# Hybrid decoder trunk on one core: first tile's gates on its own columns, query weights scaled a stage earlier, state's copy ahead of the exponential, last tile's norm by halves

## The reference

```python
# first layer, both groups from one projection of h
c_q, k_a, v_a, k_i, w_i, q_b, z_f, i_b, g_b = split(h @ w_in)
q_a = rms_norm(c_q) @ w_uq                       # queries of the attention heads
# attention: per query the 256 best keys of an index score, softmax with ALiBi
logits = (q_a . k_a) * 64 ** -0.5 - slope_h * distance
# gated recurrence (HGRN2): forget gate and key from z, per channel
logf = log(sigmoid(z_f)); k_b = sigmoid(-z_f)    # lb of the one even layer is 0
S_t = exp(logf_t) * S_(t-1) + k_t v_t ;  o_t = q_t . S_t    # S starts at 0
o = concat(o_attention, rms_norm(o_recurrent) * silu(g_b)) @ w_out
# every block
h = layer_norm(ALPHA * h + block(h)) * g + b
```

## Time and profile before

| | |
|---|---|
| Median of 3 runs | 2665.35 us (2661.79 to 2667.26) |
| Profiled execution, its own time | 2666.79 us |
| Span of its trace | 2665.0 us, mean granted clock 0.967 |
| PE busy | 2548.1 us (96%) |
| DVE busy | 1290.3 us (48%) |
| ACT busy | 844.5 us (32%) |
| POOL busy | 1063.0 us (40%) |
| HBM read, written | 215.81 MB, 12.71 MB |

### The profile page before, as it was taken

How to read it: one execution, slowest core, us unless ns; L and a number is a source line. 1 busy time by engine, 2 the same in 40 slices (tenths; PEclk the granted TensorE clock), 3 DMA queues, 4 the chain that set the end, 5 groups by cost and what they waited for, 6 DMA issues and landing times.

```text
span 2665.0 us, 36229 instructions
## 1 busy us (share of the span) xinstructions
PE 2548.1 (96%) x14090; PEld 2180.5 (82%) x14090; DVE 1290.3 (48%) x2460; ACT 844.5 (32%) x1387; POOL 1063.0 (40%) x624
## 2 busy tenths in 40 slices
PE   7899999789999989999999999999999999999996
PEld 6789999667788778899888777888787888888885
DVE  6789999588886423333333323332232332232224
ACT  3675221333333223222222322322332322332221
POOL 0432213364544414344434433444433444455442
PEclk9899999699999999999999989999998999999998
DMA  4101220333233234333323223233322233333331
GB/s 133 32 17 43 89 92 19 99 92 116 87 107 96 88 103 119 96 95 95 87 72 95 80 63 95 65 110 95 95 79 79 79 101 103 94 91 103 113 103 46
DMA packets 274613, 230.87 MB, mean 87 GB/s; under 512 B 10640, under 2 KB 255440, under 8 KB 274448
## 3 DMA queue, kind: packets, MB, share of 16 engines
q1 hardware_dynamic: 266256, 220.07, 27.7%
q10 hardware_dynamic: 8192, 8.52, 0.9%
HBM read 215.81 MB, written 12.71 MB: 86 GB/s over the span
## 4 chain that ended last, share of the span: by engine, by line
PE 59%; DMA 1%; POOL 1%; DVE 1%; ACT 1%; issue 0%; POOLq 0%; SPq 0%; ACTq 0%; DVEq 0%
PE banks L1959 36%; PE banks L1975 20%; PE banks L1992 1%; PE banks L1997 1%; PE banks L2009 1%; DMA cq_raw<-in_w_up 0%; PE banks L1668 0%; DMA last_draw<-in_w_down 0%; POOL dL L1877 0%; POOL wL L1866 0%; POOL wL L1870 0%; PE banks L1994 0%; DVE y L1641 0%; DVE y L2165 0%; ACT dH L2059 0%
## 5 line engine op out<-in xcount | busy, mean ns | idle before, releaser
L1870 POOL TENSOR_TENSOR wL<-cq_raw,wH 128x2048 fp32r<-128x2048 f32 x87 | 405.7, 4664 | 565.7 <-ACT wH L2053 565.7
L1959 PE MATMUL banks<-hL,wH 128*128 128x512 f32 (+1 forms) x1760 | 618.9, 352 | 5.6 <-ACT hid L2068 5.3
L1959 PE MATMUL banks<-hH,wL 128*128 128x512 f32 (+1 forms) x1760 | 618.0, 351 | 0.0
L1959 PE MATMUL banks<-hH,wH 128*128 128x512 f32 (+1 forms) x1760 | 616.1, 350 | 0.0
L2145 DVE TENSOR_TENSOR hid<-hid,banks 128x512 f32<-128x512 f32 (+1 forms) x110 | 64.3, 585 | 742.8 <-PE banks L1959 639.2
L1959 PEld LDWEIGHTS banks<-hL,wH 128*128 128x128 f32 x1760 | 331.3, 188 | 54.9 <-ACT hid L2068 6.5
L1959 PEld LDWEIGHTS banks<-hH,wL 128*128 128x128 f32 x1760 | 331.2, 188 | 46.4
L1959 PEld LDWEIGHTS banks<-hH,wH 128*128 128x128 f32 x1760 | 331.8, 189 | 44.9
L1877 POOL TENSOR_TENSOR dL<-last_draw,dH 128x1024 fp32r<-128x1024 f32 x88 | 220.8, 2509 | 350.6 <-ACT dH L2059 350.6
L2165 DVE TENSOR_TENSOR y<-y,banks 128x512 f32<-128x512 f32 (+1 forms) x340 | 233.1, 686 | 219.9 <-PE banks L1975 218.8
L1975 PE MATMUL banks<-dH,hidL 128*128 128x512 f32 (+1 forms) x748 | 303.9, 406 | 2.3 <-issue 2.3
(11 more groups left out here) (249 smaller groups left out, 4248.0 us busy)
## 6 DMA issues: line engine op xcount, KB each, us to landing
cq_raw<-in_w_gate SPq DMA_DIRECT2D x88, 512.0 KB, 4.6
cq_raw<-in_w_up SPq DMA_DIRECT2D x88, 512.0 KB, 6.0
last_draw<-in_w_down SPq DMA_DIRECT2D x88, 512.0 KB, 3.4
w_out_part<-in_w_out SPq DMA_DIRECT2D x60, 512.0 KB, 4.0
va<-in_w_in SPq DMA_DIRECT2D x10, 1024.0 KB, 5.5
va<-in_x SPq DMA_DIRECT2D x8, 512.0 KB, 4.4
vg_scratch<-y ACTq DMA_DIRECT2D x32, 128.0 KB, 1.7
y<-in_x SPq DMA_DIRECT2D x8, 512.0 KB, 7.5
```

Of the source, the lines that this page charges most:

```text
L1870: nc.gpsimd.tensor_tensor(wL[:, ff % 2, :, :, :].rearrange("p g k f -> p (g k f)"), raw[:, :, :, :].rearrange("p g k f -> p (g k f)"), wH[ ...
L1959: last = nc.tensor.matmul(banks[:, GU + (2 * q + g) % 3, 0:n], wt[:, ff % 2, g, k, :], h[:, k, a:a + n], start=(k == 0 and part == 0), sto ...
```

## The change

Four edits.

1. **First tile's gates.** For tile 0 the gate sub-steps work on that tile's own 16 columns per 128 (64 of 512). The padding memsets of z and q on GpSimd and SP's waits for them go; VectorE sets one key buffer to zero instead, and `S` is set to zero behind the first gate step. For tile 0 `out` leaves out the products with the state, which is zero.
2. **Query weights.** They are loaded in the projection stage into a free row of y and scaled there by ScalarE, in front of its last eight evacuations. `qa` of tile 0 reads them there and is done first in the mixers' stage; a copy by DMA from SBUF to SBUF serves the other tiles. SP waits for the copy and for `qa` of tile 0 before it loads y.
3. **State's copy.** In step h = 3 ScalarE copies the state before the exponential, as it already did with the job of step 5.
4. **The end.** ScalarE copies the last gain row into two PSUM banks during phase 3; VectorE reads it from there. The last tile's gain and bias are both done by VectorE, by halves of 512 columns, and each half is stored by itself.

```diff
+w_qa0 = y[:, 2, :].rearrange("p (k f) -> p k f", k=QC)
 # projection, SP
             sp.dma_start(slab_raw(j), ...)
+            if j == len(SLABS) - 2:
+                sp.dma_start(w_qa0, ins["w_uq"][0]...).then_inc(w_qa_loaded, 16)
 # projection, ScalarE
                 out_of_bank(m)
+                if m == len(slab_units) - 8:
+                    act.wait_ge(w_qa_loaded, 16)
+                    for h in range(A_HEADS):
+                        at = w_qa0[:, :, h * HD:(h + 1) * HD]
+                        nc.scalar.activation(at, at, ACT.Copy, scale=HD ** -0.5 / SLOPES[h]).then_inc(w_qa_scaled, 1)
 # mixers, SP
-        sp.dma_start(w_qa[:, :, :], ins["w_uq"][0]...).then_inc(w_loaded, 16)
-        sp.wait_ge(pads, 1)
         load_z(0)
-        sp.wait_ge(pads, 2)
         load_q(0)
-        sp.wait_ge(pads, 5)
+        sp.dma_start(w_qa[:, :, :], w_qa0).then_inc(w_loaded, 16)
+        sp.wait_ge(pads, 3)
         load_v(0)
 ...
         n0.load(sp, ins["ln_mix_g"][0], ins["ln_mix_b"][0])
+        sp.wait_ge(w_loaded, 16)
+        sp.wait_ge(shared_psum, nth["qa", 0])
         for m in range(5):
             load_y(m)
 # mixers, GpSimd
-        nc.gpsimd.memset(zt[:, :], PAD_Z).then_inc(pads, 1)
-        nc.gpsimd.memset(qt[:, :], 0.0).then_inc(pads, 1)
-        nc.gpsimd.memset(qp[:], 0.0).then_inc(pads, 1)
         nc.gpsimd.memset(vt[:, 0, :], 0.0).then_inc(pads, 1)
         nc.gpsimd.memset(gt[:, :], 0.0).then_inc(pads, 1)
+        nc.gpsimd.memset(qp[:], 0.0).then_inc(pads, 1)
 # mixers, TensorE
-                        nc.tensor.matmul(..., qp[:, s, par, ...], state[...], start=True, stop=False)
+                        if m:
+                            nc.tensor.matmul(..., qp[:, s, par, ...], state[...], start=True, stop=False)
-                        last = nc.tensor.matmul(..., S[:, s, h, :], vt[...], start=False, stop=True)
+                        last = nc.tensor.matmul(..., S[:, s, h, :], vt[...], start=(m == 0), stop=True)
 ...
+        on_shared("qa", 0)
         gram(0, 0)
-        on_shared("qa", 0)
 # mixers, ScalarE
+            if m == 0:
+                z, ut, lt, kt, k_in, to = own(z), own(ut), own(lt), own(kt), own(k_in), own(to)
 ...
-        gates(0, 2)
-        gates(0, 3)
-        act.wait_ge(w_loaded, 16)
-        for h in range(4):
-            scaled(h)
-        gates(0, 4)
-        gates(0, 5)
-        for h in range(4, A_HEADS):
-            scaled(h)
+        for stage in (2, 3, 4, 5):
+            gates(0, stage)
         off_shared("qa", 0)
 ...
-            early = shared_job(m, h) if h == 5 else None
+            early = shared_job(m, h) if h in (3, 5) else None
 # mixers, VectorE
-        for dst in (qaT, S):
-            nc.vector.memset(dst[:], 0.0).then_inc(dve_pads, 1)
+        nc.vector.memset(key[:, 0, :], 0.0).then_inc(dve_pads, 1)
+        nc.vector.memset(qaT[:], 0.0).then_inc(dve_pads, 1)
 ...
         gates(0, 4)
+        nc.vector.memset(S[:], 0.0).then_inc(dve_pads, 1)
 # ScalarE's evacuation of qa of tile 0
-                    act.wait_ge(dve_pads, 2)
+                    act.wait_ge(dve_pads, 3)
 # trunk
+gain_bank = banks[:, PB:PB + 2, :].rearrange("p b f -> p (b f)")
+            if ph.nth == 3 and i == HALF + 2:          # ScalarE
+                act.wait_ge(n3.gb_loaded, 32)
+                for half in range(2):
+                    nc.scalar.activation(gain_bank[:, at], n3.gb[:, at], ACT.Copy).then_inc(gain_kept, 1)
+        n3.gains_from(dve, HALF, gain_bank)            # VectorE, in the places of n3.gains
+        n3.gains_from(dve, HALF + 3, gain_bank, halves=True)
+    def gains_from(self, dve, j, gain, halves=False):  # with halves:
+        for half in range(2):
+            at = slice(half * 512, (half + 1) * 512)
+            self.nc.vector.tensor_tensor(self.y[:, m, at], self.y[:, m, at], gain[:, at], ALU.mult).then_inc(self.gained_half, 1)
+            dve.wait_ge(self.gained_half, half + 1)
+            self.nc.vector.tensor_tensor(self.y[:, m, at], self.y[:, m, at], self.bb[:, at], ALU.add).then_inc(self.biased_half, 1)
+        for half in range(2):                          # SP, the last tile's store
+            sp.wait_ge(n3.biased_half, half + 1)
+            sp.dma_start(out[0, t0:t0 + P, at], y[:, NT - 1, at]).then_inc(stored, 16)
```

More of the change, by code:

```diff
@@ L60 @@
 LEVELS = 7
+SLOPES = [2.0 ** (-8.0 * (h + 1) / A_HEADS) for h in range(A_HEADS)]
 ROUNDS_AHEAD = {NT - 2: 8, NT - 1: 0}
@@ L126, in build @@
                 with stage() as c:
[L127 removed]
+                    projection(nc, c, sem, sb, banks, ident, x, meta, w_in_v, ins, score, cqT, kaT, va, y, qz_dram, vg_dram, kiT, masks, w_qa0)
                 with stage() as c:
[L129 removed]
+                    mixers(nc, c, sem, sb, banks, ident, x, meta, ins, score, masks, w_qa0, cqT, kaT, va, y, qz_dram, vg_dram, raw, draw)
             hH = sb(top, "hH", [P, DC, L], F32R)
@@ L133, in build, with projection @@
             trunk(nc, c, sem, sb, banks, ident, ins, y, hH, hL, raw, draw, out)
-def projection(nc, c, sem, sb, banks, ident, x, meta, w_in_v, ins, score, cqT, kaT, va, y, qz_dram, vg_dram, kiT, masks):
+def projection(nc, c, sem, sb, banks, ident, x, meta, w_in_v, ins, score, cqT, kaT, va, y, qz_dram, vg_dram, kiT, masks, w_qa0):
     NX = 3
@@ L675, in _, with mixers @@
                 nc.vector.match_replace(at, top8[:, m, :], at, TAKEN).then_inc(late_taken, 1)
-def mixers(nc, c, sem, sb, banks, ident, x, meta, ins, score, masks, cqT, kaT, va, y, qz_dram, vg_dram, raw, draw):
+def mixers(nc, c, sem, sb, banks, ident, x, meta, ins, score, masks, w_qa0, cqT, kaT, va, y, qz_dram, vg_dram, raw, draw):
     W = 4 * P
@@ L1293, in gates @@
         def gates(m, stage):
-            z = zt[:, :]
+            z, ut, lt, kt, k_in, to = (zt[:, :], u[:, :], lnw[:, :], key[:, m % 2, :], key_arg[:, :], tot[:, m % 2, span(0)])
+            if m == 0:
+                z, ut, lt, kt, k_in, to = own(z), own(ut), own(lt), own(kt), own(k_in), own(to)
             if stage == 2:
@@ L1641, in gains @@
         self.nc.vector.tensor_tensor(self.y[0:n, m, :], self.y[0:n, m, :], self.gb[0:n, :], ALU.mult).then_inc(self.gained, 1)
+    def gains_from(self, dve, j, gain, halves=False):
+        m = self.tiles[j]
+        dve.wait_ge(self.scaled, j - self.before + 1)
+        if not halves:
+            self.nc.vector.tensor_tensor(self.y[:, m, :], self.y[:, m, :], gain, ALU.mult).then_inc(self.gained, 1)
+            return
+        for half in range(2):
[3 more added lines that the diff above has]
+            self.nc.vector.tensor_tensor(self.y[:, m, at], self.y[:, m, at], self.bb[:, at], ALU.add).then_inc(self.biased_half, 1)
     def bias(self, pool, j):
@@ L1855, in _ @@
                 store(i - 4)
-        for j in range(HALF, 2 * HALF):
+        for j in range(HALF, 2 * HALF - 1):
             store(j)
-        sp.wait_ge(stored, 16 * 2 * HALF)
+        t0 = TILES[NT - 1][0] - N_META
+        for half in range(2):
+            at = slice(half * 512, (half + 1) * 512)
+            sp.wait_ge(n3.biased_half, half + 1)
+            sp.dma_start(out[0, t0:t0 + P, at], y[:, NT - 1, at]).then_inc(stored, 16)
+        sp.wait_ge(stored, 16 * (2 * HALF + 1))
     @block.gpsimd
@@ L2235, in _, with last_adds @@
                     n2.low(dve, T - 8)
-        for T in range(HALF + 2):
-            if T < HALF:
-                for half in range(2):
-                    add(NPAIR - 1, 2 * T + half)
-                dve.wait_ge(y_added, PH[-1].down(PAIRS - 1, 2 * T + 1) + 1)
-                n3.stats(dve, HALF + T)
-            if 1 <= T <= HALF:
-                n3.factors(dve, HALF + T - 1)
-            if T >= 2:
-                n3.gains(dve, HALF + T - 2)
+        def last_adds(T):
+            for half in range(2):
+                add(NPAIR - 1, 2 * T + half)
+            dve.wait_ge(y_added, PH[-1].down(PAIRS - 1, 2 * T + 1) + 1)
+            n3.stats(dve, HALF + T)
+        last_adds(0)
+        last_adds(1)
+        n3.factors(dve, HALF)
+        last_adds(2)
+        n3.factors(dve, HALF + 1)
+        dve.wait_ge(gain_kept, 2)
+        n3.gains_from(dve, HALF, gain_bank)
+        last_adds(3)
+        n3.factors(dve, HALF + 2)
+        n3.gains_from(dve, HALF + 1, gain_bank)
+        n3.factors(dve, HALF + 3)
+        n3.gains_from(dve, HALF + 2, gain_bank)
+        n3.gains_from(dve, HALF + 3, gain_bank, halves=True)
 def kernel(**inputs):
```

59 lines of the change are left out of this document (31 added, 28 removed).

## The result

The kernel after takes 2639.45 us (median of 5 runs, 2634.59 to 2645.58) against 2665.35 before: a ratio of 0.9909, 95% interval 0.9888 to 0.9929. Run again beside other kernels it took 2643.36 us, ratio 0.9905 (0.9886 to 0.9924). Faster by 23 to 26 us; 18.5 had been forecast, to 2647 us, with a range from 2640 to 2657. The median lies half a us under the range's lower end; the ratio, taken from 2665.35 us, gives 2641.

The account below looks back on a forecast made before the run. TensorE was taken to bound the feed-forward stage, with no single bound in the mixers' stage. Terms 3.8 + 2.6 + 9.8 + 2.3 = 18.5 us gave 2648.3 us, 2647 on the median's scale; forecast 2641 to 2654, with rivals 1 and 2 2640 to 2657.

Parts of the forecast that it names:

- Start, 3.8 us: Start of the mixers' stage: z lands and gates end earlier, SP's queue sets the start; 3.8 us gained (3.0 to 4.3).
- The weights' scaling: Projection stage: eight scalings fit ScalarE's idle time before evacuations and cost nothing; without that cover two or three us.
- First output, 2.6 us: First tile's output without the state: 16 of 32 matmuls go, 3.4 us of TensorE; 2.6 us gained (0 to 3.4).
- State's copy, 9.8 us: Mixers' tiles: copy ahead of the exponential removes TensorE's stalls and VectorE's idle time; 9.8 us gained (7 to 12).
- both go on earlier by the smaller number: Tile 5's state copy: VectorE gains 4.3 us, TensorE more; the smaller, VectorE's, was taken as the gain.
- the two small ones: Two small gains from the state's copy, one in tile 7 of 0.50 us on TensorE; about 1.0 us together.
- The list of waits, 10.6 us: Mixers' stage, kernel before: TensorE's stall on the state's copy, 10.6 us in 6 waits.
- End, 2.3 us: Last tiles' norm: gain product from PSUM does not wait for GpSimd; 2.3 us gained (1.1 to 3.7).
- the wait for GpSimd at the first half's bias: End: VectorE's first-half bias reads two SBUF tiles, so it begins only when GpSimd ends, at 2656.8 us.
- The first: Rival, mixers' state copy: VectorE's own order takes the gain back, 2 of 9.8 us stay; 2655 us, chance 0.20.
- the second: Rival, start and end: z no earlier, halves wait for GpSimd twice; gains shrink to 0 and 1; 2652 us, chance 0.08.
- The third: Rival, TensorE's clock in the mixers: half clock lasts longer, using up 18.5 us or reaching 2687 us; chance 0.08.

Follow-up runs that it names:

- keep_product: The kernel after, but the first tile's output keeps its sixteen products with the empty state: 2641.45 us, ratio 0.9906 to the kernel before.
- q1_early: The kernel after with tile 1's q loaded right behind its z, ahead of the residual's loads: 2640.91 us, ratio 0.9906 to the kernel before.
- the parts alone: state_only, start_only and tail_only, each against the kernel before: 12.0, 6.75 and 3.3 us less, 22.1 us together.
- start_only: The change without the state's early copy and with the old end, against the kernel before: 2658.60 us, ratio 0.9975.
- tail_only: The kernel before with the new end of the last norm alone: 2662.01 us, ratio 0.9988 to the kernel before.
- state_only: The kernel before with only the state's copy moved ahead of that step's exponential: 2653.39 us, ratio 0.9954 to the kernel before.
- after_again: The kernel after measured once more, unchanged: 2643.36 us, ratio 0.9905 to the kernel before.

## Why the prediction was right, and where its terms were off

**Start, 3.8 us: measured 4.3.** The chain was as worked out, in stage time: z lands at 2.0 us (2.4 said), the gates end at 3.6 (3.8), the meta values go out at 5.9 (6.1), the logits come at 6.1 (6.4), the second q lands 4.5 us earlier. keep_product puts 1.9 of the 6.2 us at the first output down to the product, which leaves 4.3. In keep_product VectorE reads the first tile's product 4.3 us earlier than before, too. That SP's queue decides is shown by q1_early. The weights' scaling cost nothing: ScalarE does all eight in 1.70 us at 459.21 us, and the next evacuation still waits 0.86 us for TensorE (2.46 at the others).

**First output, 2.6 us: measured 1.9.** TensorE saved the 3.4 us of the count, and VectorE, whose wait of 2.64 us is gone, reads the product 2.8 us earlier: the term was right where it was read. By the first output 0.9 us are lost again to a low clock that all four profiles with this start show, so that 1.9 came of it.

**State's copy, 9.8 us: measured 12.5, the mis-sized term.** The first-order sizes were exact: 4.4 for 4.3 in tile 5, 2.9 for 2.85 in tile 6. The step that failed is "both go on earlier by the smaller number". Each of the six steps gained TensorE's own number, its stall and what its clock lost behind it, 11.8 us in all, and in tiles 3 to 6 that is the larger one. VectorE gains its idle time at once, and 0.4 to 0.7 us more a quarter later, where it waits for TensorE, which had won more. In tiles 3 and 4 I took VectorE's 0.8 each for what came to 1.2 and 1.6 (TensorE's 1.3 and 1.4); tile 5 gave 5.1 for 4.3, tile 6 3.4 for 2.85, the two small ones 1.2 for 1.0. The list of waits, 10.6 us, and the 1.5 us of slower product would have given the term.

**End, 2.3 us: measured 2.95.** Every row came as said, the wait for GpSimd at the first half's bias among them. The last result is ready 2.6 us nearer to the end of the gate and up products than SP's last issue was before, and a last store of half the size ends the span 0.35 us sooner.

**Sum.** 4.3 + 1.9 + 12.5 + 2.95 = 21.7 us against 18.5 forecast, and 22.1 by the parts alone. The profiled pair's 29.4 us holds more: 2.6 us of low clock at one step of the mixers, which the profile of before has and that of after has not, 6.9 us of the feed-forward stage, whose time varies from 1631.7 to 1640.6 us in these profiles with the same matmuls, less 2.1 at the first stage. What remains between 21.7 and the medians' 25.9 and 23.1 is within their spread; that no part of it belongs to the change is not shown. A part may: the low clock behind tile 6's stall, 2.8 us in start_only and 1.5 in tail_only, goes with the early copy, and the profile of before does not have it. All four mechanisms stood, so the direction and the rough size are not luck; the sum came out low mainly by the state's copy.

**Rivals.** The first (VectorE takes the state's gain back) falls by state_only, the second by start_only and tail_only. The third (half clock held longer) went the other way at the place in question: the clock rose at 39 us of stage time, 50 before. In small it came true 20 us later, at the 0.9 us in front of the first output.

## What to carry to other kernels

Where two engines in turn are the late one, size a removed stall on both and look one step further on: at the state's copies the stage gained what TensorE had stalled, not the smaller of the two idle times. Then look at the engine's clock behind the gaps that stay: at the first output it took 0.9 of 2.8 us back. A small transfer that an engine waits for should be placed in the queue by its consumer, not by its loop: moving one 256 KB load ahead of the residual's won 3.1 us at the first product, against 4.3 for the whole rework of the start. When a unit's time falls and the span does not, look at who issues its result.

## What the runs showed of the hardware that was not expected

The granted clock of TensorE differs between executions of one kernel in stretches of some 7 us (before) to 10 us (state_only), also where the engine was busy 5.00 of 5 us: 0.65 in the kernel before and 1.00 in tail_only with the same code, at the same place, and 0.50 in state_only and after_again in the step behind, which cost them 5.0 us each. Behind one and the same stall of 3.17 us it stayed full in before (a product of 3.72 us) and fell in start_only (6.56) and tail_only (5.24). Terms of a few us have to be read at steps between such stretches, not from medians.

A 32 KB transfer in pieces of 64 bytes landed 2.0 us after its issue when it was first in the queue, and 3.0 behind 512 KB.
